# Pair products of a gated linear scan: prefix sums of logarithms in 8 levels per token tile, against products of gates by doubling with both token tiles in one product per level

## The reference

```python
f = sigmoid(hf);  g = lb + (1 - lb) * f;  kk = 1 - g          # gates, keys
q = silu(hq) * 128 ** -0.5
# per head: S_t = diag(g_t) S_{t-1} + kk_t v_t^T,   o_t = S_t^T q_t
...
scores = einsum('bhtk,bhtsk,bhsk->bhts', qc, decay, kc)       # decay = exp(b_t - b_s), b = cumsum(log g), s <= t
o = rms_norm(o, hg_norm_w) * silu(hg)
```

## Time and profile before

| | |
|---|---|
| time, median of 3 runs (lowest, highest) | 2818.52 us (2818.43, 2818.69) |
| span of the profiled execution | 2816.4 us |
| its own time | not listed apart from the three; the span and some 2.1 us around it make the median |
| PE busy | 2798.3 us, 99% |
| PE weight loads busy | 2401.9 us, 85% |
| DVE busy | 2096.5 us, 74% |
| ACT busy | 1509.7 us, 54% |
| GpSimd busy | 106.8 us, 4% |
| mean rate of the DMAs | 185 GB/s |

### The profile page before, as it was taken

The page is one execution under the profiler, slowest core; times in us unless marked ns, Lnnn a source line. Parts: engine busy times, 40 slices in busy tenths (PEclk is TensorE's granted clock), DMA queues, the critical chain, the costliest instruction groups (busy, mean ns, idle before and its releaser), DMA issues.

```text
span 2816.4 us, 40938 instructions
## 1 busy us (share of the span) xinstructions
PE 2798.3 (99%) x15630; PEld 2401.9 (85%) x15630; DVE 2096.5 (74%) x3071; ACT 1509.7 (54%) x2231; POOL 106.8 (4%) x104
## 2 busy tenths in 40 slices
PE   9999999999999999999999999999999999999998
PEld 6888888888888888888888888888888888888886
DVE  5688788888677777777786676778768777777775
ACT  5556665565444444444465555556555555555554
POOL 0000000000100000000050000000000000000000
PEclk9999999999999999999999999999999999999999
DMA  7545454455565555555565655555555555555553
GB/s 270 182 161 170 156 175 159 163 172 189 178 203 186 188 194 188 187 193 188 185 217 191 193 168 189 183 171 186 187 197 194 186 192 189 192 189 189 192 190 131
DMA packets 157154, 522.19 MB, mean 185 GB/s; under 512 B 28960, under 2 KB 31392, under 8 KB 156704
## 3 DMA queue, kind: packets, MB, share of 16 engines
q1 hardware_dynamic: 155808, 517.31, 55.3%
q10 hardware_dynamic: 1152, 2.27, 0.2%
HBM read 517.42 MB, written 2.10 MB: 184 GB/s over the span
## 4 chain that ended last, share of the span: by engine, by line
PE 99%; DMA 0%; DVE 0%; ACT 0%; issue 0%; SPq 0%; ACTq 0%; DVEq 0%
PE acc L407 39%; PE acc L412 19%; PE psX L407 5%; PE psT L407 5%; PE acc_first L407 5%; PE psT L412 3%; PE psX L412 3%; PE acc_first L412 2%; PE psA L540 1%; PE acc L440 1%; PE acc L442 1%; PE acc L441 1%; PE psT L707 1%; PE psE L707 1%; PE psA L709 1%; PE psE L709 1%
## 5 line engine op out<-in xcount | busy, mean ns | idle before, releaser
L1227 DVE TENSOR_TENSOR w_lo<-w_raw,w_hi 128x1024 fp32r<-128x1024 f32 x958 | 1170.9, 1227 | 356.0 <-ACT w_hi L782 326.7
L782 ACT ACTIVATE w_hi<-w_raw 128x1024 fp32r<-128x1024 f32 x958 | 1003.0, 1055 | 488.7 <-PE acc L407 218.4
L407 PE MATMUL acc<-XU,w_hi 128*128 128x512 f32 x2848 | 926.8, 397 | 0.0
L412 PEld LDWEIGHTS acc<-XU,w_lo 128*128 128x128 f32 x2848 | 535.2, 188 | 124.6
L407 PE MATMUL acc<-XY,w_hi 128*128 128x512 f32 x1792 | 579.1, 398 | 0.0
L412 PE MATMUL acc<-XU,w_lo 128*128 128x256 f32 x2848 | 560.1, 278 | 0.0
L407 PEld LDWEIGHTS acc<-XU,w_hi 128*128 128x128 f32 x2848 | 446.9, 189 | 6.4 <-issue 2.6
L412 PEld LDWEIGHTS acc<-XY,w_lo 128*128 128x128 f32 x1792 | 336.7, 188 | 77.9
L412 PE MATMUL acc<-XY,w_lo 128*128 128x256 f32 x1792 | 352.6, 278 | 0.0
L407 PEld LDWEIGHTS acc<-XY,w_hi 128*128 128x128 f32 x1792 | 278.7, 189 | 8.2 <-issue 5.3
L787 ACT ACTIVATE cross<-acc 128x256 f32<-128x256 f32 x242 | 92.5, 382 | 309.8 <-PE acc L407 309.8
(11 more groups left out here) (356 smaller groups left out, 3447.6 us busy)
## 6 DMA issues: line engine op xcount, KB each, us to landing
w_raw<-in_weights SPq DMA_DIRECT2D x962, 512.0 KB, 3.4
bias<-in_rel_bias SPq DMA_DIRECT2D x8, 384.0 KB, 3.8
bias<-in_rpb_back SPq DMA_DIRECT2D x32, 96.0 KB, 5.8
hT<-in_x_t SPq DMA_DIRECT2D x8, 256.0 KB, 7.7
G<-in_norm_rows SPq DMA_DIRECT2D x2, 1024.0 KB, 8.0
out_dram<-G SPq DMA_DIRECT2D x2, 512.0 KB, 4.0
out_dram<-G ACTq DMA_DIRECT2D x2, 384.0 KB, 4.5
G<-in_range_sums ACTq DMA_DIRECT2D x1, 576.0 KB, 4.3
```

The costliest lines, as they stand in the source:

```text
L407: return nc.tensor.matmul(bank[:, :], hi[:, k, col:col + P], X[:, k0 + k, :], start=first and k == 0, stop=last and k == nk - 1 and k % 2 ...
L412: return nc.tensor.matmul(bank[:, 0:T], lo[:, k, col:col + P], X[:, k0 + k, 0:T], start=False, stop=last and k == nk - 1 and k % 2 == 0, s ...
L782: act.activation(w_hi[s][:, 0:n], w_raw[s][:, 0:n], ACT.Copy).then_inc(hi_done, 1)
L1227: V.tensor_tensor(w_lo[s][:, 0:n], w_raw[s][:, 0:n], w_hi[s][:, 0:n].bitcast(F32), ALU.subtract).then_inc(lo_ready, 1)
```

## The change

In `heads1` the logarithm, its transpose, the range sums, the exponentials and GpSimd's product go. Instead DVE keeps running products of gates. `HS[:, 0]` holds four rows of 128: keys of tile 0, queries times gates of tile 1, queries times gates of tile 0, keys of tile 1. Tile 1 is held last token first (`turned`), so that what is "later" in tile 0 is "earlier" in memory in tile 1, and one product of gathered rows serves both tiles at a level. At level n (blocks of z = 2^n tokens) PE makes one product (`level_products`), DVE then multiplies half of the entries by the gate product of the neighbouring block (`widen_spans`), gathers the stationary operand of the next level (`gather_keys`), halves the list of gate products, and takes level n's pairs out of PSUM by a predicated copy under a mask (`take_pairs`). PE's level n + 1 waits for `widen_spans(n)`, and `widen_spans(n)` waits for PE's level n. The level products stand behind the blocks 5 to 11, one a block, and `tile_pairs` behind block 12.

In `vals1`, since the second tile's values of the scan must come last token first as well, the attention's values are made first, ACT turns the activation's second tile into `XY` in blocks 4 to 7 (8 copies of 128 x 512), and one more token sum is made. The masks are 15 instead of 9, the 9 range sums are no longer loaded. Cut to its core:

```diff
@@ two_blocks
+        KQ = HS[:, 0, :, :].rearrange("p a t -> p (a t)")
+        GT = HS[:, 1, :, :].rearrange("p a t -> p (a t)")
+        def spans(n):
+            return GT[:, 2 * T - (2 * T >> n):2 * T - (T >> n)]
+        def hs_view(offset, dims):
+            return bass.AP(tensor=KQ.tensor, offset=KQ.offset + offset, ap=[KQ.ap[0], *dims])
+        def pair_bank(n):
+            return psE if n % 2 else psA
+        def turned(x):
+            return x[:, T - 1:P - 1:-1]
...
@@ tensor
-            def decays(k):
...
-                    nc.tensor.matmul(psE[:, :], lg_hi[:, a, :], rhs, start=True, stop=False)
-                    nc.tensor.matmul(psE[:, :], lg_lo[:, a, :], rhs, start=False, stop=True).then_inc(S("decay_full"), 1)
...
+            def level_products(n):
+                def job(i):
+                    pe.wait_ge(S("kq_ready"), (LEVELS + 1) * i + n + 1)
+                    if n >= 2:
+                        pe.wait_ge(S("pairs_taken"), LEVELS * i + n - 1)
+                    z, nb, bank = 1 << n, P >> (n + 1), pair_bank(n)
+                    done = nc.tensor.matmul(bank[:, 0:P], HS[:, 3, 0, :], hs_view(P, [[2 * z, nb], [P + z, 2], [1, z]]), start=True, stop=True)
+                    if n == 0:
+                        for a in range(NT):
+                            done = nc.tensor.matmul(bank[:, (a + 1) * P:(a + 2) * P], HS[:, 0, 3 * a, :], HS[:, 2, a, :],
+                                                    start=True, stop=True)
+                    done.then_inc(S("pairs_full"), 1)
...
             after1 = {
-                4: [transpose_pair(wk(0), "lg_ready", "lgT_full")],
-                6: [decays(0)],
-                8: [pair_products(0), decays(1)],
-                10: [pair_products(1), decays(2)],
-                11: [scores(0, P, 1)],
-                12: [pair_products(2), decays(3)],
+                5: [level_products(0)],
+                6: [level_products(1)],
+                7: [level_products(2)],
+                8: [level_products(3)],
+                9: [level_products(4)],
+                10: [level_products(5)],
+                11: [scores(0, P, 1), level_products(6)],
+                12: [tile_pairs],
                 13: [scores(1, T, 1)],
-                14: [pair_products(3), tile_pairs],
...
@@ scalar
+                if 4 <= b < KB:
+                    four = slice(4 * b - 2 * KB, 4 * b - 2 * KB + 4)
+                    act.wait_ge(x_first, b - 3)
+                    for n in range(2):
+                        ins = act.activation(XY[:, four, n * P:(n + 1) * P], XU[:, four, n * T:(n + 1) * T][:, :, T - 1:P - 1:-1].bitcast(F32), ACT.Copy)
...
-                        act.activation(HS[:, 0, :, :], psE[:, :], ACT.Exp).then_inc(S("decay_exp"), 1)
...
@@ vector
             def gate_query(i):
...
+                link(V.scalar_tensor_tensor(HS[:, 2, 0, :], wk(2)[:, 0:P], HG_SCALE, wk(4)[:, 0:P], ALU.mult, ALU.mult))
+                mark(V.scalar_tensor_tensor(HS[:, 2, 1, :], turned(wk(2)), HG_SCALE, turned(wk(4)), ALU.mult, ALU.mult), S("q_ready"), i + 1)
+                link(V.tensor_tensor(HS[:, 0, 2:0:-1, :], HS[:, 2, 0:NT, :], HS[:, 1, 0:NT, :], ALU.mult))
+                mark(gather_keys(0), S("kq_ready"), (LEVELS + 1) * i + 1)
+
+            def gather_keys(n):
+                z, nb = 1 << n, P >> (n + 1)
+                return V.tensor_copy(HS[:, 3, 0, :].rearrange("p (b h i) -> p h b i", h=2, i=z),
+                                     hs_view(0, [[3 * P + z, 2], [2 * z, nb], [1, z]]))
...
+            def widen_spans(n, i):
+                z, nb = 1 << n, P >> n
+                both = [[T + z, 2], [2 * z, nb], [1, z]]
+                dve.wait_ge(S("pairs_full"), LEVELS * i + n + 1)
+                ins = V.tensor_tensor(hs_view(0, both), hs_view(0, both),
+                                      hs_view(spans(n).offset - KQ.offset + 1, [[-1, 2], [2, nb], [0, z]]), ALU.mult)
+                if n < LEVELS - 1:
+                    link(ins)
+                    ins = gather_keys(n + 1)
+                mark(ins, S("kq_ready"), (LEVELS + 1) * i + n + 2)
+                if n < LEVELS - 1:
+                    old = spans(n).rearrange("p (b h) -> p h b", h=2)
+                    link(V.tensor_tensor(spans(n + 1), old[:, 0, :], old[:, 1, :], ALU.mult))
+
+            def take_pairs(n, i):
+                bank, both = pair_bank(n), AT[:, 0:3:2, :]
+                if n == 0:
+                    eye = masks[:, 0:1, :].bitcast(mybir.dt.uint16).to_broadcast([P, NT, P])
+                    link(V.copy_predicated(both, eye, bank[:, P:3 * P].rearrange("p (a t) -> p a t", a=NT)))
+                source = bank[:, 0:P].rearrange("p (a t) -> p a t", a=1).to_broadcast([P, NT, P])
+                mark(V.copy_predicated(both, masks[:, 1 + 2 * n:3 + 2 * n, :].bitcast(mybir.dt.uint16), source),
+                     S("pairs_taken"), LEVELS * i + n + 1)
...
+                    n = b - 6
+                    if 0 <= n < LEVELS:
+                        widen_spans(n, i)
                     if b != 14:
                         low_part(p, i, b)
+                    if 0 <= n < LEVELS:
+                        take_pairs(n, i)
```

More of the change, by code:

```diff
@@ L31 @@
 NREL_COLS = 384
+LEVELS = 7
 RPB_BACK = RPB_R * RPB_C - 1 - (10 * RPB_C + 63 + 15)
@@ L173, in two_blocks @@
     nc, weights, x_t, columns, conv_columns, hg_norm, rel_bias, w_s_t, mix_bias, norm_rows, rpb_back,
-    range_sums, pair_masks, identity, window, out,
+    pair_masks, identity, window, out,
 ):
@@ L484, in _ @@
                 else:
[L485 removed]
+                    value_products(p, b, XU, val_banks[c % 2], lambda k: (x_first, k // 4 + 1), turn=c % 2 == 1)
                 if b == 9:
[L487 to L488 removed]
+                    pe.wait_ge(S("sq_first"), 2)
+                    token_sums(0, 0)
+                    nc.tensor.matmul(psT[:, NT:NT + 1], sqacc[:, 1, 0:P], ones[:, 0:1], start=True, stop=True).then_inc(S("tok_sum"), 1)
                     rms_sum()
@@ L809, in value_tile @@
                 bank = val_banks[c % 2][a][:, :].rearrange("p (h n) -> p h n", h=4)
-                h0, kind = c // 2 * 4, c % 2
+                h0, kind = c // 2 * 4, 1 - c % 2
+                scale = mix_rs[:, 2:3] if a and kind == 0 else mix_rs[:, a:a + 1]
                 near = 4 if c < 2 else 3
                 ins = act.activation(G[:, KD + 2 * h0 + kind:KD + 2 * (h0 + near - 1) + kind + 1:2, a * P:(a + 1) * P],
-                                     bank[:, 0:near, :], ACT.Copy, scale=mix_rs[:, a:a + 1])
+                                     bank[:, 0:near, :], ACT.Copy, scale=scale)
                 if near == 3:
-                    ins = act.activation((v_nat, av_nat)[kind][:, a, :], bank[:, 3, :], ACT.Copy, scale=mix_rs[:, a:a + 1])
+                    ins = act.activation((v_nat, av_nat)[kind][:, a, :], bank[:, 3, :], ACT.Copy, scale=scale)
                 ins.then_inc(S("vals_out"), 1)
@@ L893, in _ @@
                         sigmoid_of(0, "hf_z", "hf_sig", i)
-                    if b == 2:
-                        act.wait_ge(S("g_ready"), i + 1)
-                        act.activation(wk(0), wk(0), ACT.Ln).then_inc(S("lg_ready"), 1)
+                    if b and b % 2 == 0 and b not in (14, 16):
                         round_next(p, i, b)
@@ L1173, in _ @@
             nc.gpsimd.memset(ones[:, :], 1.0).then_inc(S("ones_set"), 1)
-            p = ph["heads1"]
-            for i in range(p.iters):
-                for b in range(p.blocks):
-                    if b in (6, 8, 10, 12):
-                        k = (b - 6) // 2
-                        pool.wait_ge(S("decay_exp"), i * 4 + k + 1)
-                        if k == 0:
-                            pool.wait_ge(S("g_ready"), i + 1)
-                        else:
-                            pool.wait_ge(S("pairs_full"), i * 4 + k)
-                        kk = wk(1)[:, (k // 2) * P:(k // 2 + 1) * P].rearrange("p (a t) -> p a t", a=1)
-                        nc.gpsimd.tensor_tensor(HS[:, 2, :, :], HS[:, 0, :, :], kk.to_broadcast([P, 4, P]), ALU.mult)\
-                          .then_inc(S("kE_ready"), 1)
             def out_projection(name, n0):
@@ L1327, in _ @@
                     lower_bounds()
+            link(V.memset(AT[:, :, :], 0.0))
+            dve.wait_ge(S("masks_set"), 1)
             p = ph["heads1"]
@@ L1724, in shape_constants @@
     s_, t_ = t[:, None], t[None, :]
-    sums = np.zeros((9, P, P), np.float32)
-    masks = np.zeros((9, P, P), np.float32)
-    sums[0] = s_ > t_
-    sums[8] = s_ <= t_
-    masks[0] = masks[8] = np.eye(P)
-    for l in range(7):
-        z = 1 << l
-        mid = t_ // (2 * z) * (2 * z) + z
-        upper = t_ % (2 * z) >= z
-        sums[l + 1] = np.where(upper, (s_ >= mid) & (s_ <= t_), (s_ > t_) & (s_ < mid))
-        masks[l + 1] = (s_ // (2 * z) == t_ // (2 * z)) & (s_ % (2 * z) < z) & upper
+    masks = np.zeros((2 * LEVELS + 1, P, P), np.float32)
+    masks[0] = np.eye(P)
```

(4 more changed lines are left out.)

116 lines of the change are left out of this document (24 added, 92 removed).

## The result

| | before | after |
|---|---|---|
| time, median | 2818.47 us (4 runs, 2818.13 to 2818.69) | 2795.2 us (4 runs, 2794.46 to 2795.99) |
| span of the profiled execution | 2816.4 us | 2793.3 us (its own time 2795.07) |
| one head, from one product to the same one of the next head | 60.34 us | 57.39 us |

The ratio is 0.9917, with a 95% interval of 0.9906 to 0.9929: 23.3 us faster. The forecast was 2797.4, in a range from 2792 to 2811. One execution of `e2_both` (4745.66 us) and one of `e3_take2` (3917.16 us) ran at a granted clock of 0.63 and 0.65 where all others have 0.998 or 0.999; the ratios leave them out, and the medians hardly move by them.

A forecast was written before the change was run, and what follows sets the result against it. PE, busy for 99% of the span, was taken as the bound. Its work shrinks by 26.1 us, less 0.2 for `vals1` and 4.8 of waits: 21.1 off, time 2797.4 us, range 2792 to 2811.

The forecast's parts named there:

- That only PE's row counts: Whole kernel: PE fills 99% of the span, so other engines count only where they make PE wait.
- What PE loses, 5.96 us a head: Heads: transposes, range sums, pair products and the five products behind block 14 leave PE's row, 5.96 us a head.
- What PE gains, 2.70: Heads: new small products behind blocks 5 to 12 cost PE 2.70 us a head, with 0.09 per group for returning to weights.
- a rival of 1.6 us in all: Level-0 product: PE reads the two tiles slowly, 0.2 us a head, 1.6 in all, time 2799.0; chance 0.12.
- The prices of DVE: Heads, new DVE operations: widening 0.42 us, gather 0.23, predicated copy 0.42 with upper bound 0.69.
- That DVE's total would stay where it was: Heads: new DVE operations sum to about 10 us a head against 10.8 removed.
- The wait, and its place: Heads: PE waits for DVE only behind block 12, for `tile_pairs`; 0.4 to 0.76 us a head, 0.6 taken, 4.8 in all.
- the list of margins for blocks 6 to 12: Heads: us by which DVE is early when PE asks, block by block, from 1.20 at block 6 to -0.36 at 12.
- The slope, 0.7 us a head for each 0.1 us in every level: Heads' level loop: each 0.1 us more of DVE in every level adds 0.7 us a head.
- it becomes slower: Level loop: waits exceed PE's 3.26 us gain a head, from 0.42 more a level; 2828 us; chance 0.05, another 0.05 near break-even.
- `vals1` at +0.2: Value phase `vals1`: one added fp32 token sum costs PE at most 0.21 us, once; the copies on ACT cost 0.
- What lies around the span, 2.1 us and unchanged: Outside the profiled span: the median exceeds the span by 2.1 us, and this does not change.

The follow-up runs named there:

- e2_both: Against the changed kernel, `tile_pairs` moved to the scores' group behind block 13 and DVE's output-gate product from block 6 to block 15; 0.990, median 2791.12 us.
- e3_take2: Against the changed kernel, each level's predicated copy made twice, 0.48 us more DVE in each of 7 levels; 0.9998, median 2818.74 us.

## Why the prediction was right

It forecast 21.1 us less and 23.3 were measured. The mechanism is the one it gave; the sizes of two terms were off in the same direction. By its steps:

- **That only PE's row counts**: right, by the account that closes (2.96 against 2.95) and by the run without the low range sums (8.0 for an expected 7.5).
- **What PE loses, 5.96 us a head**: right. It could be read off the trace of before, since PE had no wait there.
- **What PE gains, 2.70**: 2.57, which is 1.0 us of the miss. Two errors in it cancel in part. A single product between weight blocks costs 0.22 to 0.24, not 0.30: the 0.09 for returning to the weights, read from groups of four and five, is not there for a lone product that came with time to spare. It is there for one that was waited for: 0.32 and 0.33. And level 0 costs 0.78, not 0.71, of which the scattered read is 0.10 by experiment; the prediction had held that as a rival of 1.6 us in all. It is 0.8, and taking it out brings nothing, because PE then comes too early behind block 8.
- **The prices of DVE**: the widening 0.426 (0.42 taken), the gather 0.228 (0.23), the predicated copy 0.443 (0.42, upper bound 0.69). The one missed is the gate operation with a per-channel scalar, 0.343 for 128 elements instead of 0.29; it lies in block 2, where there was cover. That DVE's total would stay where it was did not hold: it fell by 2.8 us a head, which no term of the sum uses.
- **The wait, and its place**: the list of margins for blocks 6 to 12 was 1.20, 0.63, 0.18, 0.44, 0.04, 1.08, -0.36, with the wait behind block 12 alone. In the trace they are, read in the same way from the ends on DVE and the starts on PE, 1.28, 0.62, 0.12, 0.32, -0.13, 1.09 and -0.30: a second wait of 0.13 stands behind block 10. The list was too kind to blocks 8 to 10 by up to 0.17, above all since each lone product is 0.07 cheaper than the 0.30 taken, so that PE asks sooner. The total of 0.43 lies close to the sum's 0.4, which is in part luck: one wait was overlooked and the other taken too long. The prediction took 0.6 a head from a sum that gave 0.4 to 0.76. This allowance is the largest single miss, 1.4 us.
- **The slope, 0.7 us a head for each 0.1 us in every level**: 0.48 us in each level made 2.93, the list and slope give 0.39 + 0.7 x 4.8 = 3.7 of wait, so some 3.3 more than the 0.4. Of the 2.93, 2.70 are waits and the rest dearer products behind them. Right in kind, but too steep by a fifth for this edit: the second copy of block 12 stands behind the last widening, where no product of the loop waits for it, so only six of the seven count, 2.88 at most, and a part of that is used up by margins. The rival "it becomes slower" had its break-even at 0.42 us more a level; measured, it is just about 0.48.
- **`vals1` at +0.2**: 0.21. The copies were hidden.
- **What lies around the span, 2.1 us and unchanged**: 1.8 (2795.07 against 2793.3), another 0.3 of the miss. Why it fell is open.

## What to carry to other kernels

When one engine is busy to 99%, count what leaves its row and what comes to stand on it, and then walk the new chain of waits block by block with the other engine's order of work. The other engine's share of busy time (83% here) says nothing on it: 0.48 us added in each of the seven levels cost the whole gain, and 0.48 us a head taken out of the loop gave 3.9 us back. In such a loop, release the waiting engine first and do everything else behind it, and move what nobody waits for (a gate product, a product whose result is used three blocks later) out of the blocks whose margin is smallest.

A small saving in a loop that already waits, or is close to it, is not seen at all (the scattered read), and over a third of an added cost can be hidden (the second product per level, 1.06 paid of 1.7): try such edits only after the waits are gone. A margin just above nothing is not enough either. The weight load goes ahead of its product, and when the operands come in time for the product but not for the load, the product costs 0.10 us more without any wait to be seen before it.

## What was not expected of the hardware

- A lone fp32 product of 128 columns between products of 512 costs 0.22 to 0.24 us of PE's time, and 0.32 to 0.33 if PE had to wait for it. It costs nearly as much (0.29 to 0.33) when only its weight load comes late: behind block 8 without the scattered read, and behind block 12 without the gate product in the loop. The same product in a row of several costs about 0.21 each.
- A moving operand that jumps 516 bytes and back at each column costs 0.10 us more for 128 columns in fp32; in pairs of neighbouring floats (level 1) the product costs 0.24 in all, next to nothing more.
- An operand with one value per partition (here one per channel or one per token) has a price on DVE that does not grow with the number of elements: a TENSOR_SCALAR of 256 takes 0.295 us with constants alone (L1279), 0.352 with one such operand (L1320) and 0.406 with two (L1290 of the kernel before). For 128 elements it is 0.286 with one (L1320) and 0.343 with two (L1278). So each costs some 0.06 us. That explains the gate operation's 0.343, and the 0.48 of the output-gate product (L1372, one such operand) against 0.42 for the same operation with a constant (L1286 of the kernel before).
